# A decoder step with window attention, a recurrence and 32 experts: biases turned early and picked by register, norm parameters out of the ring, cache loads after the tenth tile, two ScalarE functions behind evictions

## The reference

```python
proj = x @ p['w_in']                  # 1024 -> 6144: q, k, v, rnn-x, rnn-y, gate_attn, gate_rnn
o_attn, nk, nv = attend(q, k, v, p['attn_sinks'])       # window 128, 16 heads, sinks; the sample reads its caches
xc = causal_conv(xr)                  # width 4
r = sigmoid(xc @ wa + ba); i = sigmoid(xc @ wx + bx)    # ten blocks of 128
log_a = (-8.0 * softplus(-lam)) * r
a = exp(log_a); b = sqrt(-expm1(2.0 * log_a)) * (i * xc)
h_t = a_t * h_(t-1) + b_t             # scan over the positions
y_rnn = h * gelu(yr)
merged = sigmoid(ga) * (o_attn @ w_attn_out) + sigmoid(gb) * (y_rnn @ w_rnn_out)
x = layer_norm(alpha * x + merged @ w_out, ln1_g, ln1_b)
# top 4 of 32 experts, softmax over the four logits; for each expert e and its tokens:
h = xblk @ w_up[e] + b_up[e];  glu, lin = h[:, :1024], h[:, 1024:]
glu = minimum(glu, 7); lin = clip(lin, -7, 7)
y += gate * ((glu * sigmoid(1.702 * glu) * (lin + 1)) @ w_down[e] + b_down[e])
x = layer_norm(alpha * x + y, ln2_g, ln2_b)
```

## Time and profile before

| What | Value |
|---|---|
| Median of 3 runs | 1358.52 us |
| Fastest and slowest | 1355.88 and 1358.93 us |
| The profiled execution, and its span | 1356.15 and 1354.3 us |
| PE busy | 1266.5 us (94%), 5886 matmuls |
| DVE busy | 437.1 us (32%), 784 instructions |
| ACT busy | 218.0 us (16%), 447 instructions |
| Moved by DMA | 450.16 MB, mean 332 GB/s |
| Granted TensorE clock, mean | 0.98 |

### The profile page before, as it was taken

The page is one execution under the profiler, slowest core; times in us unless marked ns, Lnnn a source line. Parts: engine busy times, 40 slices in busy tenths (PEclk is TensorE's granted clock), DMA queues, the critical chain, the costliest instruction groups (busy, mean ns, idle before and its releaser), DMA issues.

```text
span 1354.3 us, 15851 instructions
## 1 busy us (share of the span) xinstructions
PE 1266.5 (94%) x5886; PEld 600.4 (44%) x5886; DVE 437.1 (32%) x784; ACT 218.0 (16%) x447; POOL 21.3 (2%) x25
## 2 busy tenths in 40 slices
PE   7999899999699999999999999999999999999993
PEld 6888787884353343343233224323332432342230
DVE  0474346123622322422222332222223222222326
ACT  1244363100201011110011101000110100011110
POOL 1000000000000000000000000000000000000003
PEclk9999999999789999999999999999999999999997
DMA  9622343367069999999999999999999999999991
GB/s 294 206 94 71 98 152 113 97 204 311 5 260 419 420 419 419 419 421 420 420 421 421 421 421 421 421 421 420 421 421 420 421 421 421 421 420 421 420 418 46
DMA packets 100167, 450.16 MB, mean 332 GB/s; under 512 B 7627, under 2 KB 48331, under 8 KB 50926
## 3 DMA queue, kind: packets, MB, share of 16 engines
q1 hardware_dynamic: 98992, 446.93, 82.0%
q0 software_dynamic: 784, 2.57, 0.6%
q10 hardware_dynamic: 358, 0.21, 0.1%
HBM read 448.35 MB, written 2.45 MB: 333 GB/s over the span
## 4 chain that ended last, share of the span: by engine, by line
SPq 52%; PE 35%; issue 4%; DVE 4%; DMA 4%; ACT 1%; DVEq 0%
SPq L514 32%; SPq L516 17%; PE hidden L1107 6%; PE hidden L892 5%; PE bank L892 4%; PE bank L1124 3%; PE hidden L974 2%; PE bank L974 2%; DMA rawl<-in_w_down 2%; DMA raw<-in_w_in 2%; PE bank L1070 2%; DVE xrp L1318 1%; PE share L1138 1%; PE bank L995 1%; PE share L995 1%
## 5 line engine op out<-in xcount | busy, mean ns | idle before, releaser
L1107 PE MATMUL hidden<-rawl,xg 128*64 128x512 f32 x1368 | 321.9, 601 | 10.2 <-DMA rawl<-in_w_up 9.4
L1592 DVE TENSOR_TENSOR xtok<-xtok,share 128x1024 f32<-128x1024 f32 (+1 forms) x97 | 118.1, 1217 | 401.3 <-PE share L1138 386.5
L1107 PEld LDWEIGHTS hidden<-rawl,xg 128*64 128x64 f32 x1368 | 88.7, 136 | 200.4 <-issue 139.7
L1107 PE MATMUL hidden<-raw,xg 128*64 128x512 f32 x680 | 162.0, 602 | 13.8 <-DMA raw<-in_w_up 13.0
L1124 PE MATMUL bank<-rawl,at 128*64 128x512 f32 x552 | 132.5, 600 | 4.7 <-DMA rawl<-in_w_down 3.6
L1563 DVE TENSOR_TENSOR glin<-turned,bup 128x512 f32<-128x512 f32 x64 | 44.0, 688 | 276.4 <-PE turned L1082 276.4
L775 ACT ACTIVATE hsb<-hidden 128x512 f32<-128x512 f32 x64 | 34.7, 596 | 547.7 <-PE hidden L1107 547.7
L1124 PE MATMUL bank<-raw,at 128*64 128x512 f32 x472 | 113.2, 601 | 6.9 <-DMA raw<-in_w_down 3.4
L1138 PE MATMUL share<-ysb,gt 64*128 64x512 f32 x376 | 103.0, 625 | 0.9 <-ACT ysb L784 0.9
L892 PE MATMUL hidden<-xT,raw 128*128 128x264 f32 x384 | 92.3, 399 | 6.5 <-DMA raw<-in_w_in 4.1
L1107 PEld LDWEIGHTS hidden<-raw,xg 128*64 128x64 f32 x680 | 44.1, 136 | 115.4 <-issue 84.9
(11 more groups left out here) (321 smaller groups left out, 935.7 us busy)
## 6 DMA issues: line engine op xcount, KB each, us to landing
rawl<-in_w_up SPq DMA_DIRECT2D x171, 1024.0 KB, 26.2
raw<-in_w_up SPq DMA_DIRECT2D x85, 1024.0 KB, 26.2
rawl<-in_w_down SPq DMA_DIRECT2D x69, 1024.0 KB, 26.5
raw<-in_w_down SPq DMA_DIRECT2D x59, 1024.0 KB, 26.2
raw<-in_w_in SPq DMA_DIRECT2D x23, 1024.0 KB, 5.4
raw<-in_w_rnn_out SPq DMA_DIRECT2D x8, 640.0 KB, 4.4
raw<-in_w_attn_out SPq DMA_DIRECT2D x4, 1024.0 KB, 5.0
raw<-in_w_out SPq DMA_DIRECT2D x4, 1024.0 KB, 4.8
```

Source lines behind the costliest of these rows:

```text
L1107: last = pe.matmul(hidden[h * CAP:(h + 1) * CAP, s, :], xg[:, k, i % GB, :], moe_slot(e, f"u{k}")[:, n * 512:(n + 1) * 512], start=k == 0, ...
L1592: dve.tensor_tensor(xtok[0:n, t, :], xtok[0:n, t, :], frm[t][0:n, :, :].rearrange("p h n -> p (h n)"), ALU.add).then_inc(added, 1)
```

## The change

It has five parts.

1. b_up is loaded as chunk 21 of the first ring, between the chunks of ga and gb. Behind the tile ga 6 TensorE turns all of it (16 transposes of 32 rows) into bank 4, and ScalarE evicts it to bupT, 1 added to the second half (biasturn). The products biases(0) and biases(1) and VectorE's copy of them go. In each expert VectorE reads the expert's number from tablei into a register, and the bias add takes column number "block" of bupT. For the first four blocks the number is fixed.
2. ln1's two rows leave the ring for the memory of xg, and are loaded after y_rnn_ready, behind the last load of w_out.
3. POOL's loads and copies wait for tile_done 10 in place of x_turned 5.
4. The exponentials of the sample's softmax move on ScalarE from behind yr 9 to behind r 6; the root moves from behind ga 5 to behind gb 0.
5. The clearing of xl's last block moves on VectorE behind the copies of gateT.

Places in memory were exchanged so that these fit (ga, xg and bdown).

```diff
@@ -112,10 +112,12 @@
...
     section("ga", off_ga, D)
+    chunks.append(("bup", 0))
     section("gb", off_gb, D)
     placed = {("yr", 8): ("sample", 0), ("yr", 9): ("sample", 1), ("i", 9): ("sample", 2), ("ga", 0): ("sample", 3),
-              ("ga", 1): ("gate", 0), ("ga", 3): ("oturn", 0), ("ga", 5): ("gate", 1)}
+              ("ga", 1): ("gate", 0), ("ga", 3): ("oturn", 0), ("ga", 5): ("gate", 1), ("ga", 6): ("biasturn", 0), ("r", 6): ("exps", 0),
+              ("gb", 0): ("gate", 2)}
     order = []
@@ -130,14 +132,15 @@
...
     chunks += [("wao", 256 * i) for i in range(4)] + [("wro", P * i) for i in range(8)]
-    chunks += [("wout", 2 * i) for i in range(4)] + [("ln1", 0), ("bup", 0)]
+    chunks += [("wout", 2 * i) for i in range(4)]
     return chunks, tiles, order, n_tiles_chunks
...
     NCH = len(chunks)
-    CH_AO, CH_RO, CH_OUT, CH_LN, CH_BUP = NPC, NPC + 4, NPC + 12, NPC + 16, NPC + 17
+    CH_AO, CH_RO, CH_OUT = NPC, NPC + 4, NPC + 12
+    CH_BUP = chunks.index(("bup", 0))
     NT1 = len(tiles)
@@ -249,20 +253,20 @@
...
         rawl = sb("rawl", [P, MOE_RING - RING, SLOT], scope=late)
+        xg = sb("xg", [P, KD, GB, CAP], scope=late)
         xh = sb("xh", [P, 3, D], F32R, scope=late)
         xl = sb("xl", [P, 3, D], F32R, scope=late)
+        bdown = sb("bdown", [NE, D], scope=late)
         onehot = sb("onehot", [P, 3, GB, CAP], F32R, scope=late)
-        bup = sb("bup", [P, 2, 4, 2, NB], scope=late)
-        xg = sb("xg", [P, KD, GB, CAP], scope=late)
         at = sb("at", [P, 4, 2, CAP], scope=late)
...
         ysb = sb("ysb", [P, 512], scope=late)
-        bdown = sb("bdown", [NE, D], scope=late)
         glin = sb("glin", [P, 2, 8, CAP], scope=late)
...
         late.close()
+        ln1 = xg[:, :, :, :].rearrange("p d e c -> p (d e c)")
         s_const = sem("s_const")
@@ -383,7 +389,7 @@
         def loads(c):
-            return sum(2 if chunks[x][0] == "ln1" else 1 for x in range(c % RING, c + 1, RING))
+            return c // RING + 1
         def chunk_ready(e, c):
@@ -457,18 +463,16 @@
             def used(c):
-                if c < NPC:
+                if c == CH_BUP:
+                    sp.wait_ge(bup_turned, 1)
+                elif c < NPC:
                     sp.wait_ge(tile_done, max(n for n in range(NT1) if tiles[n][2] == c) + 1)
...
                     sp.wait_ge(out_done, 8 + c - CH_RO + 1)
-                elif c < CH_LN:
+                else:
                     sp.wait_ge(mix_done, 3)
-                elif c == CH_LN:
-                    sp.wait_ge(x1_ready, 3)
-                else:
-                    sp.wait_ge(table_done, 3)
             sp.dma_start(const[:, 0:P], a["consts"][:, 0:P]).then_inc(s_ident, 16)
@@ -490,15 +494,16 @@
...
                     pieces = [(slot(c).rearrange("p (k n) -> p k n", k=2), wout[:, at0:at0 + 2, :])]
-                elif kind == "ln1":
-                    pieces = [(slot(c)[:, 0:D], a["ln1_g"].partition_broadcast(P)),
-                              (slot(c)[:, D:2 * D], a["ln1_b"].partition_broadcast(P))]
                 else:
...
+
+            sp.wait_ge(y_rnn_ready, 1)
+            sp.dma_start(ln1[:, 0:D], a["ln1_g"].partition_broadcast(P)).then_inc(ln1_loaded, 16)
+            sp.dma_start(ln1[:, D:2 * D], a["ln1_b"].partition_broadcast(P)).then_inc(ln1_loaded, 16)
             def moe_load(e, what, row0, of=None):
@@ -561,7 +566,7 @@
...
         def _(pool):
-            pool.wait_ge(x_turned, 5)
+            pool.wait_ge(tile_done, 10)
             pool.dma_start(kc[:, :, :], a["cache_k"][0].rearrange("b w g d -> w b (g d)")).then_inc(s_cache, 16)
@@ -693,14 +698,24 @@
...
                     act.activation(ig[:, :, :], ig[:, :, :], ACT.Sigmoid).then_inc(gates_done, 1)
-                elif what == "gate":
+                elif what == "gate" and n == 1:
                     act.wait_ge(tanh_done, RT)
...
                     act.activation(yr[:, :, :], yr[:, :, :], ACT.Gelu_apprx_tanh).then_inc(gelu_done, 1)
+                elif what == "gate":
                     act.wait_ge(ratio_ready, 1)
                     act.activation(sg[:, :, :], sg[:, :, :], ACT.Sqrt, scale=2.0).then_inc(root_done, 1)
+                elif what == "biasturn":
+                    act.wait_ge(bup_turned, 1)
+                    for s in range(2):
+                        half = bank[4][:, s * 256:(s + 1) * 256].rearrange("p (h f n) -> p h f n", h=2, f=4)
+                        if s == 0:
+                            act.activation(bupT[:, s, :, :, :], half, ACT.Copy).then_inc(bup_ready, 1)
+                        else:
+                            act.activation(bupT[:, s, :, :, :], half, ACT.Identity, bias=ones[:, 0:1])\
+                                .then_inc(bup_ready, 1)
                 elif what == "oturn":
@@ -711,6 +726,10 @@
...
                             .then_inc(oT_ready, 1)
+                elif what == "exps":
+                    act.wait_ge(s_sm, 1)
+                    act.activation(slog, slog, ACT.Exp).then_inc(s_ex, 1)
+                    act.activation(srow[:, 1, :], srow[:, 1, :], ACT.Exp).then_inc(s_ex, 1)
                 elif what == "sample":
@@ -718,10 +737,6 @@
...
                                 .then_inc(s_kte, 1)
-                    elif n == 1:
-                        act.wait_ge(s_sm, 1)
-                        act.activation(slog, slog, ACT.Exp).then_inc(s_ex, 1)
-                        act.activation(srow[:, 1, :], srow[:, 1, :], ACT.Exp).then_inc(s_ex, 1)
                     elif n == 2:
@@ -917,6 +932,14 @@
...
                         weigh(n - 2)
+                elif what == "biasturn":
+                    chunk_ready(pe, CH_BUP)
+                    pe.wait_ge(oT_ready, 4)
+                    for f in range(16):
+                        c0 = f // 2 * 256 + f % 2
+                        last = pe.transpose(bank[4][:, f * NE:(f + 1) * NE], slot(CH_BUP)[0:NE, c0:c0 + 255:2],
+                                            ident[0:NE, 0:NE])
+                    last.then_inc(bup_turned, 1)
                 elif what == "oturn":
@@ -1050,15 +1073,6 @@
...
             last.then_inc(table_done, 1)
-            def biases(half):
-
-                chunk_ready(pe, CH_BUP)
-                for f in range(8):
-                    c0 = (4 * half + f // 2) * 256
-                    last = pe.matmul(bank[4 + half][:, f * NB:(f + 1) * NB],
-                                     slot(CH_BUP)[0:NE, c0 + f % 2:c0 + 256:2], selm[:, :], start=True, stop=True)
-                last.then_inc(table_done, 1)
-
@@ -1143,7 +1157,6 @@
...
                 if t == 0:
-                    pe.wait_ge(bup_ready, 2)
                     pe.wait_ge(biases_loaded, 16)
@@ -1200,9 +1213,7 @@
...
             gather((0, 0), 0, spare)
-            biases(0)
             gather((0, 0), 1, downs)
-            biases(1)
             for j in (2, 3):
@@ -1467,18 +1478,17 @@
...
                     .then_inc(xl_ready, 1)
-            chunk_ready(dve, CH_LN)
+            dve.wait_ge(ln1_loaded, 32)
             dve.wait_ge(s_bd, 32)
...
                 moments(t, mixed[t], var_ready)
-                normalise(t, sd_ready, slot(CH_LN)[:, 0:D], slot(CH_LN)[:, D:2 * D], x1_ready)
+                normalise(t, sd_ready, ln1[:, 0:D], ln1[:, D:2 * D], x1_ready)
                 if t == 1:
...
                     dve.memset(xh[:, 2, :].bitcast(F32), 0.0)
-                    dve.memset(xl[:, 2, :].bitcast(F32), 0.0)
                     low_tokens(0)
@@ -1520,6 +1530,7 @@
...
             dve.tensor_copy(gateT[:, :], bank[1][0:NE, 0:T]).then_inc(routeT_ready, 1)
+            link(dve.memset(xl[:, 2, :].bitcast(F32), 0.0))
             low_tokens(1)
@@ -1543,25 +1554,28 @@
...
             one_hot((0, 0))
-            dve.wait_ge(table_done, 3)
-            for half in range(2):
-                dve.tensor_scalar(bup[:, half, :, :, :].rearrange("p f h n -> p h f n"),
-                                  bank[4 + half][:, 0:8 * NB].rearrange("p (h f n) -> p h f n", h=2, f=4),
-                                  float(half), None, ALU.add)\
-                    .then_inc(bup_ready, 1)
             for t, (_, n) in enumerate(TILES):
...
             dve.wait_ge(bup_ready, 2)
+            dve.wait_ge(table_ready, 1)
+
+            def which(e):
+
+                if isinstance(e[0], int):
+                    return e[1]
+                return dve.value_load(tablei[0:1, bass.ds(number(e, 1, 0), 1)], min_val=0, max_val=NE - 1)
             def clamp(e):
+                block = which(e)
                 for s, limit, ready in ((0, LIMIT, glu_ready), (1, LIMIT + 1, lin_ready)):
...
                     o = glin[:, s, :, :]
-                    bias = bup[:, s, :, :, bass.ds(number(e, 1, 0), 1)].rearrange("p f h n -> p (f h) n")
-                    dve.tensor_tensor(o, turned[:, s, :].rearrange("p (f n) -> p f n", f=8),
-                                      bias.broadcast_to([P, 8, CAP]), ALU.add).then_inc(hT_taken, 1)
```

(4 more changed lines are left out.)

5 lines of the change are left out of this document (4 added, 1 removed).

## The result

The changed kernel takes 1338.62 us (median of four runs, 1337.74 to 1340.81) against 1357.2 us before (median of four, one run more than in the table above): ratio 0.9869, 95% interval 0.9853 to 0.9885. The forecast was 1336.5 us with a range of 1330 to 1344.

A forecast was written before the change was run, and what follows sets the result against it. The expert-weight stream at 421 GB/s was taken as the bound, with TensorE's path counting one for one before it. 6.2 + 4.9 + 3.4 + 2.5 + 3.5 - 0.3 = 20.2 us gain, giving 1336.5 us, range 1330 to 1344.

The forecast's parts named there:

- The bound: Whole kernel: the end moves with when the 421 GB/s expert-weight stream can run unbroken; earlier TensorE time counts one for one.
- Six loads: Ring before the first expert: six more weight loads run in a 32 us DMA gap; gain 6.2 us, bounds 2 to 8.5.
- fixed 2.0 us a transfer: Restart of the weight stream: a cost beside the bytes; paid eight times without overlap, it would leave the six loads nothing.
- marks for a wrong prediction: DMA below 400 GB/s anywhere from 400 to 1290 us, late turn period other than 119.7, or VectorE's turn wait gone.
- Caches later: Start, third w_in chunk: moving POOL's transfers removes a 3.10 us wait and 1.78 us of slow group; 4.9 us, 0 to 5.
- Exponentials: Sample softmax on ScalarE: seven r tiles evicted first, so the r and i evictions end earlier; gain 3.4 us, 1 to 4.
- Root and b_up: Gate tiles: moving the root saves 4.1 us, b_up's 16 transposes cost 1.6; net 2.5 us, 0 to 3.
- Picking biases: Between the gathers: 2 x 8 products leave TensorE; gain 3.5 us, 1.4 to 4.5, register read and strided bias free.
- rival 4: Each expert: picking the bias by register stretches the way from turn to w_down products, making the kernel slower; chance 0.02.
- Clearing xl: VectorE before copying the table's columns: the moved 0.91 us clearing costs 0.3 us, from nothing to all 0.91 and gaps.

The follow-up runs named there:

- second profile of before: The kernel before the change, run once more with nothing changed, for a second profile; 1356.78 us.
- interleaved: Changed kernel with b_down's products moved to the second expert, and gathers 3 and 4 behind the first expert's second and fourth product; 1331.74 us, ratio 0.9819 to before.
- changed family: The changed kernel and its follow-up variants, one profile each; measured times from 1330.95 to 1345.66 us.

## Why the prediction was right, point by point

- **The bound.** The end follows the start of the stream, and TensorE's path counts one for one ahead of it. Shown: the exponentials put back cost 5.6 us at their place and all of it at the end (5.9 by the spans, 5.5 by the medians). The second profile of before shows the other half: its first product comes 1.16 us earlier than in the first (386.92 against 388.08) and its stream at the same time (383.96 against 383.79); turn 23 is at 1077.24 against 1077.21.
- **Six loads**, 6.2 us forecast: 19.8 us at turn 23 less 15.2 at the first product leave 4.6. The step was right, the loss in the first expert too small: 2.3 taken from the mean spacing of eight slots, 4.1 measured. The rate stayed at 340 to 378 GB/s while slots came free one by one, and that lasted to 406 us, not 397. The fixed 2.0 us a transfer that the prediction set beside this step (the Trainium skill's section quoted there has them for transfers that GpSimd issues, these are SyncE's) would have made 16 us for eight loads; 0.5 us each were lost. One of my marks for a wrong prediction (below 400 GB/s behind 400 us) was met for these six microseconds, at 359 GB/s.
- **Caches later**, 4.9 us forecast: 3.5 us between the two profiles, and 1.4 by the experiment. What failed is that I took all of it, 3.10 + 1.78. The wait of 3.10 us was 1.6 to 1.7 in two other profiles, and the slow group stood ahead of it there, as the first one, where the changed kernel has it too. With a slow first group the move is worth 1.3 to 1.5 us. With a fast one, the profiles of before and interleaved are 5.1 us apart, near the 4.9 forecast; that is one profile of each, and whether the wait made its slow group stays open.
- **Exponentials**, 3.4 us forecast: 4.8 between the profiles, 5.6 by the experiment. I had kept the old pace of evictions, 0.505 us; behind ScalarE's short wait they ran at 0.36 to 0.45, and TensorE's granted clock is 1.00 from 155 to 170 us, where before it was 0.81 to 0.84 from 160 to 170.
- **Root and b_up**, 2.5 us forecast: 2.1. The transposes cost 2.03 us, not 1.6: 0.13 us a pass, as much as a pass of the products that they replace (2.10 for 16). The split was wrong: turning b_up early gives 1.7 of it although it adds work, since it fills the stall and the slow group behind the stall (9.05 us, 8.86 in the second profile of before) doesn't come; the move of the root gives 0.4. In three profiles out of twelve of the changed family TensorE ran a slow group just behind the transposes (65.21 in the table), which takes back 1.69 us.
- **Picking biases**, 3.5 us forecast, 1.4 to 4.5 as bounds: 5.1 us, above them, and 6.5 against the second profile of before. The clock was the mis-sized part. The sum left 8.9 us for the gathers if the clock went as before, and more if it stayed low; they took 7.89, as some seven of the 16 groups ran slow in place of nine. In the kernel before they had fallen back to 1.2 GHz behind the second set of products, as TensorE's timeline shows:

```profile
385.39 0.84 PE L1070 MATMUL bank<-onehot,xh 128*128 128x256 f32 x3
```

  Register read and strided bias cost nothing, as forecast; rival 4 has nothing left.
- **Clearing xl**, -0.3 us: -0.26, and the experiment gives it back.
- **Between turn 23 and the end** 1.4 us were lost that I had not in the sum: a slow group in the last expert. Two of the twelve profiles of the changed family are without it, so it may be chance; this stays open.

Sum by stages: 3.49 + 4.81 + 2.09 - 0.26 + 5.07 + 4.58 - 1.38 = 18.4 us. The forecast of 20.2 was near it by luck too, with errors of both signs. Measured less forecast, these are +1.4 (exponentials) and +1.6 (picking biases) against -1.4 (caches), -0.4 (root and b_up), -1.6 (six loads) and -1.4 (the end).
